# Attention weights, values and the self layer's output of a two-layer decoder transposed by DMA instead of TensorE

## The reference, cut to what matters

```python
kv = x1 @ kv_w                  # x1: output of the self layer; keys and values, 16 heads of 128
q, z = split(x1 @ b_w_in)       # queries and the SiLU gate
zz = q @ k.T * 128 ** -0.5
log_1mb = where(mask, log_sigmoid(-zz), 0)                   # mask: s < t
between = reverse_cumsum(log_1mb) - log_1mb
a = where(mask, exp(log_sigmoid(zz) + between), 0)           # weights, 2048 x 2048 per head
att = a @ v
y = layernorm(ALPHA * x1 + (att * silu(z)) @ w_out)
```

## Time and profile before

| | us |
|---|---|
| three runs, median | 2936.62 (2935.66 to 3031.54) |
| the profiled execution | 2937.9 |
| its span, slowest core | 2936.6 |
| spans of the 8 cores | 2926.6 to 2936.6 |
| granted TensorE clock, mean over the span, by core | 0.982 to 0.984 |

### The profile page before, as it was taken

One profiled execution on the slowest core, in us unless ns is written; L12 is line 12 of the kernel. 1 busy time (PEld: TensorE's weight loads), 2 busy tenths in 40 slices (PEclk: granted clock), 3 DMA queues, 4 the chain that ended last, 5 costly groups with the idle time before them and its releaser, 6 DMA issues.

```text
span 2936.6 us, 51572 instructions; the slowest of 8 cores (2926.6 to 2936.6 us)
## 1 busy us (share of the span) xinstructions
PE 2762.1 (94%) x16379; PEld 1442.2 (49%) x16379; DVE 1889.5 (64%) x3211; ACT 1407.2 (48%) x2835; POOL 408.5 (14%) x418
## 2 busy tenths in 40 slices
PE   6899999999999999999999999999999999977897
PEld 2455555555556644444444444444444444443443
DVE  3555555555554445535777877777788787787666
ACT  1344444444445534434556555555556555553211
POOL 1001000010001023321100100010010001002433
PEclk9999999999999999999999999999999999998999
DMA  9704224342133255536121111111111211132453
GB/s 138 124 10 67 38 42 78 52 67 39 23 53 54 49 170 176 176 108 116 31 37 28 35 30 35 30 30 35 28 35 30 37 28 33 24 97 94 146 172 129
DMA packets 66645, 200.05 MB, mean 68 GB/s; under 512 B 7632, under 2 KB 32080, under 8 KB 60752
## 3 DMA queue, kind: packets, MB, share of 16 engines
q0 software_dynamic: 16848, 92.35, 19.7%
q1 hardware_dynamic: 49536, 104.41, 10.8%
HBM read 239.00 MB, written 50.07 MB: 98 GB/s over the span
## 4 chain that ended last, share of the span: by engine, by line
PE 73%; DVE 12%; issue 6%; ACT 4%; DMA 3%; DVEq 0%; ACTq 0%; POOL 0%; SPq 0%; POOLq 0%
PE PS L864 25%; PE PS L312 14%; PE PS L581 10%; PE PS L466 7%; DVE M L975 5%; PE PS L598 5%; PE PS L1015 3%; PE PS L953 3%; DVE M L485 3%; PE PT L996 2%; DVE M L983 2%; PE PS L996 1%; ACT M L956 1%; DMA M<-y 1%; ACT M L477 1%
## 5 line engine op out<-in xcount | busy, mean ns | idle before, releaser
L864 PE MATMUL PS<-M 128*128 128x512 bf16 x4096 | 988.2, 382 | 2.5 <-ACT M L384 1.9
L975 DVE TENSOR_TENSOR_SCAN M<-M 128x513 f32<-128x513 f32 (+3 forms) x640 | 745.7, 1167 | 315.2 <-ACT M L956 304.7
L864 PEld LDWEIGHTS PS<-M 128*128 128x128 bf16 x4096 | 386.5, 98 | 424.9 <-issue 46.1
L581 PE MATMUL PS<-M 128*128 128x512 bf16 x2048 | 487.0, 381 | 9.4 <-ACT M L589 9.4
L956 ACT ACTIVATE M<-PS 128x512 f32<-128x512 f32 (+3 forms) x640 | 342.8, 537 | 285.5 <-PE PS L953 222.0
L312 PE MATMUL PS<-M 128*128 128x512 bf16 x2048 | 460.1, 384 | 5.7 <-DVE M L1024 4.8
L983 DVE TENSOR_TENSOR M<-M 128x512 bf16<-128x512 f32 (+3 forms) x640 | 370.1, 598 | 0.0
L312 PEld LDWEIGHTS PS<-M 128*128 128x128 bf16 x2048 | 200.5, 99 | 245.6 <-issue 18.2
L581 PEld LDWEIGHTS PS<-M 128*128 128x128 bf16 x2048 | 189.3, 98 | 216.7 <-issue 17.3
L466 PE MATMUL PS<-M 128*128 128x512 bf16 x1024 | 245.1, 387 | 28.6 <-DMA M<-a_qk 16.6
L257 POOL TENSOR_TENSOR M<-M 128x1 f32<-128x1 f32 x160 | 87.8, 549 | 1166.9 <-DVE M L665 862.6
(11 more groups left out here) (131 smaller groups left out, 2706.7 us busy)
## 6 DMA issues: line engine op xcount, KB each, us to landing
M<-b_wp POOLq DMA_DIRECT2D x64, 512.0 KB, 5.2
y<-M SPq DMA_DIRECT2D x64, 512.0 KB, 3.2
M<-a_g POOLq DMA_DIRECT2D x8, 2048.0 KB, 17.5
M<-x SPq DMA_DIRECT2D x32, 512.0 KB, 5.0
M<-y SPq DMA_DIRECT2D x32, 512.0 KB, 4.9
M<-xT POOLq DMA_DIRECT2D x8, 1024.0 KB, 12.2
M<-a_qk POOLq DMA_DIRECT2D x16, 512.0 KB, 9.7
M<-a_v POOLq DMA_DIRECT2D x8, 1024.0 KB, 23.2
```

Source lines behind the costliest of these rows:

```text
L581: kb.op("pe", lambda: P_.matmul(PS[1][:, :], lhsT=XTv[:, t // 4, c, (t % 4) * 128:(t % 4 + 1) * 128], rhs=WAG[h % 2][:, c, :], start=(c == ...
L864: kb.op("pe", lambda: P_.matmul(PS[bank][:, :], lhsT=WR[w][:, c, :], rhs=XTv[:, tb, c, :], start=(c == 0), stop=(c == KC - 1)), R=[("WR", ...
L975: kb.op("dve", lambda: V.tensor_tensor_scan(out=rev(P[ps], 512 - w, 513), data0=rev(U[us], 512 - w, 513), data1=d1, initial=init, op0=ALU. ...
```

## The change

The transposes of the attention weights, of V and of the self layer's output become DMA transposes from SBUF to SBUF, issued from SP. There is one per tile of attention weights (128 x 128 to 128 x 512, 640 in all), one per V block (128 x 512, 64 in all) and one per row tile of the self layer's output (128 x 2048, 16 in all). The ScalarE copies from PSUM behind them go too. AT becomes three buffers of a whole unit each, A six buffers in place of nine; `trans` of unit k now stands in step k, not k+1. The quota is 65 pulls a head. Bank 6, which the transposes used, becomes a third bank for the projections. `b_wo` is loaded in 16 pieces in place of 8, 10 of them at the start, and in the last head's steps the loads of y and stores of the output are issued by GpSimd in place of SP.

```diff
+    def dmat(self, slot, out, in_, R=(), W=()):
...
+        self._deps("sp", R, W)
+        ent = self.dsem[slot]
+        ent[1] += 16
+        self.eng["sp"].dma_start_transpose(out=out, in_=in_).then_inc(ent[0], 16)
...
             def xt_stage(self, t):
                 p = t % 2
-                for g in range(2):
-                    tbuf, tkey = [(PT[:, :], "PT"), (PSB0, ("ps", 0))][g]
-                    for j in range(8):
-                        c = g * 8 + j
-                        kb.op("pe", lambda: P_.transpose(out=tbuf[:, j * 128:(j + 1) * 128],
...
-                    kb.op("act", lambda: A_.copy(out=XTv[:, t // 4, g * 8:(g + 1) * 8, (t % 4) * 128:(t % 4 + 1) * 128],
...
+                kb.dmat(f"x1t{p}", XTv[:, t // 4, :, (t % 4) * 128:(t % 4 + 1) * 128], self.XB[p],
+                        R=[("XB", p, 0), ("XB", p, 1)], W=[("X1T", t)])
...
-        NU, NP, NA, NAT = 3, 5, 9, 3
+        NU, NP, NA, NAT = 3, 5, 6, 3
...
                         kb.op("act", lambda: A_.copy(out=VT[:, bsl], in_=PS[bank][:, :]),
-                              R=[("ps", bank)], W=["VT"])
+                              R=[("ps", bank)], W=[("VT", tb)])
+                        kb.dmat(f"vt{tb}", VVs[par][:, 4 * tb:4 * tb + 4, :], VT[:, bsl], R=[("VT", tb)],
+                                W=[("VV", par, tb)])
...
-        pbank[0] = [4, 5]
+        pbank[0] = [4, 5, 6]
...
-        def trans(k, pr):
+        def trans(k, i):
             h, gq, sb_, diag, ws = lanes(k)
...
+            n = k * 4 + i
+            as_, w, at = n % NA, ws[i], k % NAT
+            kb.dmat(f"tr{as_}", AT[at][:, 0:w // 128, i * 128:(i + 1) * 128], A[as_][:, 0:w], R=[("Ab", as_)],
+                    W=[("AT", at, i)])
...
             opB.pool_add = True
+            opB.q = "pool"
...
-                quota = 67 * (pos + 1) // 10 - 67 * pos // 10
+                quota = 65 * (pos + 1) // 10 - 65 * pos // 10
...
                 sub(k, 0)
-            if 0 <= k - 1 < NUN:
-                trans(k - 1, 0)
+                trans(k, 0)
             fill(1)
...
                 sub(k, 1)
+                trans(k, 1)
...
                 sub(k, 2)
+                trans(k, 2)
                 sub(k, 3)
-            if 0 <= k - 1 < NUN:
-                trans(k - 1, 1)
+                trans(k, 3)
             fill(3)
```

More of the change, by code:

```diff
@@ L123, in dma @@
         self._record(("d_" + slot, ent[1]), R, W)
+    def dmat(self, slot, out, in_, R=(), W=()):
+        if slot not in self.dsem:
+            s = self.es.enter_context(self.nc.semaphore("d_" + slot))
+            self.dsem[slot] = [s, 0]
+            self.semobj["d_" + slot] = s
+        self._deps("sp", R, W)
+        ent = self.dsem[slot]
+        ent[1] += 16
+        self.eng["sp"].dma_start_transpose(out=out, in_=in_).then_inc(ent[0], 16)
+        self._record(("d_" + slot, ent[1]), R, W)
     def barrier(self):
@@ L282, in __init__ @@
                 self.pool_add = False
+                self.q = "sp"
                 self.fin = []
@@ L367, in finish @@
                       R=keys + [self.tag + "LNB"], W=keys)
-                kb.dma("sp", f"{self.tag}y{i}{hf}", y_out[t * 128:(t + 1) * 128, hs], seg, R=keys, W=[("y", t, hf)])
+                kb.dma(self.q, f"{self.tag}y{i}{hf}{self.q}", y_out[t * 128:(t + 1) * 128, hs], seg, R=keys, W=[("y", t, hf)])
                 if self.xt_out:
@@ L810, in build @@
         KTs = [mv(136 * K + 4 * K * i, S) for i in range(2)]
-        VVs = [mv(144 * K + 4 * K * i, S, BF16, ("VV", i)).rearrange("p (t n) -> p t n", t=NT) for i in range(2)]
-        VT = mv(152 * K, S, BF16, "VT")
+        VVs = [mv(144 * K + 4 * K * i, S).rearrange("p (t n) -> p t n", t=NT) for i in range(2)]
+        VT = mv(152 * K, S)
         for i in range(2):
@@ L816, in build @@
                 kb.reg(("KTs", i, tb), 136 * K + 4 * K * i + K * tb, K)
+                kb.reg(("VV", i, tb), 144 * K + 4 * K * i + K * tb, K)
+        for tb in range(4):
+            kb.reg(("VT", tb), 152 * K + K * tb, K)
         MS = [mv(156 * K + K * i, 512, BF16, ("MS", i)) for i in range(3)]
@@ L889, in proj_stream @@
                     yield None
[L890 to L902, removed]
                     if kind == "Z" and tb == 3:
@@ L1015, in av @@
                 kb.op("pe", lambda: P_.matmul(PS[obank][:, f0:512], lhsT=VVs[par][:, sb_ * 4 + j, :],
[L1016 removed]
+                                              rhs=AT[at][:, j, f0:512],
                                               start=(diag and j == 0), stop=last, skip_group_check=True),
[L1018 removed]
+                      R=[("VV", par, sb_)] + [("AT", at, i) for i in range(j if diag else 0, 4)], W=[("ps", obank)], inc=(jj == 1))
             if sb_ == 0 and pr == 1:
@@ L1058, in need_mid_b @@
             return [("MIDG", (t // 4) % 2), ("MIDX", (t // 4) % 2)]
-        opB = OutProj(y_out, b_ln_g, b_ln_b, lambda nb, c: WOB[2 * nb + c // 8][:, c % 8, :],
-                      lambda nb: [("WOB", 2 * nb), ("WOB", 2 * nb + 1)],
+        opB = OutProj(y_out, b_ln_g, b_ln_b, lambda nb, c: WOB[4 * nb + c // 4][:, c % 4, :],
+                      lambda nb: [("WOB", 4 * nb + i) for i in range(4)],
                       lambda t, c: MIDG[(t // 4) % 2][:, c, (t % 4) * 128:(t % 4 + 1) * 128], need_mid_b,
@@ L1067, in build @@
         need(0)
-        for i in range(6):
+        for i in range(10):
             ld_wob(i)
@@ L1082, in build @@
                         pre_load(0)
-                        ld_wob(6)
-                        ld_wob(7)
+                        for i in range(12, 16):
+                            ld_wob(i)
                         pre_load(1)
```

52 lines of the change are left out of this document (18 added, 34 removed).

## The result

The changed kernel takes 2979.8 us (four runs, 2977.5 to 2982.3), the one before 2936.5: ratio 1.0148, 95% interval 1.0129 to 1.0168. It is slower by 43 us. The forecast was 2787 us and faster. In the experiments some runs had the four cores of one die at a lower clock and are left out; e9 has one run left and so no interval, and the trace of e10 is read on the other die.

A forecast was written before the change was run, and what follows sets the result against it. TensorE's queue was taken as the attention bound, VectorE close behind; 2937.9 − 151.5 (fifteen heads) − 14 (self layer's output) + 15 (crowded stretches) = 2787 us; own range 2735 to 2835, whole range 2735 to 3000.

The forecast's parts named there:

- Rival A: Attention part, SP's one queue: transposes bound at 2.8 us per 128x512, 106.4 us a head, 3241 us; chance 0.20.
- Rival B: Attention heads: VectorE takes the bound fully, no run-ahead; 81 us a head if A·V also waits, 2859 us; chance 0.16.
- part 4: Starts of cross layer and last head: loads crowd the transposes; worst 25 + 30 us, 15 taken for both.
- the work of a head: TensorE in a head: 70.0 us of matmuls plus 8.5 of transposes, 78.5 of the 85.3 us.
- The price of the DMA transposes: SP's queue: 38 equivalents at 1.7 us, 65 us a head, hidden under 75.2, so priced at nothing.
- Latency: Transposed tile to A·V, one step (7.5 us) later: 2 us of issue and landing fit, as does 3.9 us VectorE lag.
- TensorE's run-ahead: Attention units: TensorE can run some three tiles, about 6 us, ahead, carrying much of VectorE's excess.
- Rival C: Attention heads: four b_wp loads make transposes late, 10 us a head come back, about 2937 us; chance 0.14.
- Removed waits: TensorE ahead of weight and V transposes: 2.3 + 1.2 = 3.5 us of waits a head go.
- part 2: Self layer's output, transposes among the output projection's matmuls moved to DMA: 14 us gained.
- The 1.9 us of backlog: Three full units in series: VectorE, slower than TensorE, builds up 1.9 us, charged once a head, giving 75.2 us.

The follow-up runs named there:

- e9: Changed kernel with A·V one unit later, ten b_wo loads spread over heads 1 to 10, no TensorE waits on its own semaphore, nothing left out: 2845.6 us.
- e10: e9 with the last head's loads issued one after another: 2822 to 2828 us, ratio 0.9612.
- e12: e10 with A·V collected by turns in two PSUM banks, bank 3 and the one the transposes left free: 2717 to 2723 us, ratio 0.9254.
- e6: Changed kernel with A·V one unit later and a fourth AT buffer, one b_wo piece left out for room: 2886 us, ratio 0.9827.
- e5: Changed kernel with only the first four of the 64 b_wp loads issued: 2919 us, ratio 0.9941.
- e4: Changed kernel with the ten first b_wo loads spread over heads 1 to 10: 2966 us, ratio 1.0097.
- e7: Changed kernel without three loads at the last head's start (both LayerNorm rows, second mid_b block): 2956 to 2960 us, ratio 1.0072.
- e11: e9 but with TensorE again waiting on its own semaphore: 2882.7 us, ratio 0.9807.
- e1: Kernel before with only the self layer's output transposed by DMA: 2923.5 us, ratio 0.9953.

## Why the prediction was wrong

The direction was wrong. That 2980 us lies inside the range up to 3000 is no merit: what lies above 2835 in it belongs to the rivals. The lower end, 2735, is a slip in the sum (2787 less 28 and 15 is 2744), and rivals A and B left out the 15 us of part 4; neither changes the reading.

**What bounds the kernel, the work of a head.** Right. 70.0 us of matmuls were worked out; e12 runs a head in 70.8. VectorE's 68 us a head stayed too (950 us in 14 heads of e12). The 8.5 us of transposes are read from the trace; no run takes them apart.

**The price of the DMA transposes.** Right that the queue keeps up. That 65 us of SP's queue a head were forecast and 65 measured is luck. The forecast took 38 landings of 1.7 us one after another; the trace has 44 transposes at 1.5 us each, of which 1.19 is the issue, hardly less when the tile is narrow (least 1.12), and landings of 2.4 us that overlap. Rival A, with its break-even at 2.24 us of service, did not happen. Its packets did come, 364,512 more on this queue, some 540 for each 128x512; but by the queue's shares of 16 engines' span, 27.4% after and 10.8% before, a further packet took 0.022 us (an estimate), not 0.102.

**Latency: the step that failed.** The prediction said that A·V reads the last tile "one step (7.5 us) later. Issue and landing, 2 us, fit, and so does a VectorE lag of two tiles (3.9 us)." Each term was given its usual size, and each was held against the 7.5 us alone. They add up: the VectorE lag of two tiles 3.9, a landing of 2.4, another transpose or two of 1.2 to 1.5 ahead in the queue make 7.5 to 9.3 (an estimate), and there is no room for a landing of 7.9 beside a b_wp load. In the wait shown above 6.0 us were left from the subtraction to A·V's turn, and 1.7 in the queue and 7.9 of landing had to fit. e6 gives one unit more and takes back 93 us. Of the 9.8 us that a head missed (85.0 for 75.2) this is the largest part, 5.1; the own wait is 2.3, and what was left after both (77.0 in e9) went with the second bank. I had also let TensorE's run-ahead carry VectorE's excess for free; that the same slack can't be spent on both is argued, no run separates the two.

**Contention.** Rival C had the mechanism, four b_wp loads a head that make a transpose late, and priced it at 10 us a head; e5 shows 4.2. Part 4 had its places right and its size wrong: 15 us for both stretches, where head 0 lost 26 and head 15 lost 40. e4 and e7 confirm the causes for head 0 and for half of head 15. "Best case nothing, worst one such landing each time" (25 and 30 us) held for head 0, which has one such wait, of 25.3 us; head 15 has two, of 19.9 and 26.2.

**The own wait.** Not in the prediction at all, so put at nothing. I counted the transposes as work on TensorE and didn't ask what they covered. It costs 2.3 us a head once A·V is in time (79.3 in e11, 77.0 in e9), and up to 37 us in all.

**Removed waits and part 2.** The 3.5 us of waits did go. The self layer's part was 14 us by e1, as forecast.

**Rival B, VectorE.** The 1.9 us of backlog was not needed: e12 has no such loss. The real limit of that kind was the single A·V bank, which has TensorE wait for VectorE's product; it was named ("one product with the gate (0.68 us) per query group on top") as VectorE's load only and not as a wait of TensorE's.

**Open.** Why two banks give 6.1 us a head where the wait was 5.6: likely the run-ahead that it allows, not tried apart. What holds head 15 at 125 us in e12, with VectorE's share at 73%, was not tried; its trace still has two waits of 11 us for a transposed tile there. Why four of e9's cores start later than the other four is open. The kernel before was not run with two A·V banks, since it has no free bank.

## What to carry to other kernels

When work moves from an engine to the DMA queues, its throughput is the easy half: ask how long one result may take in its worst neighbourhood, and give the consumer a whole stage more than the sum of lag, queue and landing, or the moved work's gain comes back as waits (here at a lower clock as well). Before instructions are removed, look at what they covered; a wait that cost nothing behind them costs its full price when they go. And spend what the change sets free, here a PSUM bank, on the wait that is now the dearest.

## What was not expected of the hardware

A transpose from SBUF to SBUF takes SP 1.12 to 1.19 us to issue, whether 128 or 512 columns wide, where a plain DMA takes 0.32; it lands in 2.2 us at the least, and at the latest, between 1400 and 2500 us, in 8.8; the one of 7.9 us had one 512 KB load beside it. In e12, where the queue is fuller, the latest of heads 1 to 14 took 17.1. Plain stores of mid_b behind transposes took 0.52 us to issue and 2.6 to land (0.32 and 1.7 before). After 3.8 us without work TensorE's next ten matmuls took 3.48 us from start to start (2097.30 to 2100.78): the two of A·V and the first projection still came some 0.2 us apart, then they came 0.43 us apart, the 1.2 GHz level. The Trainium skill, page "DMA: Bandwidth & Descriptors", section "Rules for kernel authors", says that a transpose next to ordinary DMAs needs nothing. That holds for what it computes; for when it lands, this trace shows up to 26 us of waiting.
